# Two fused transformer blocks on one core: work of the first microseconds shared out among three engines, and three waits before matmuls put in another order

## The chip, the cores and the metric

The kernel runs on one NeuronCore of a Trainium2 chip: a matrix engine (TensorE, PE in the profile), a vector engine (VectorE, DVE), an activation engine (ScalarE, ACT), a general one (GpSimd, POOL) and a sync engine (SyncE, SP) which here only issues transfers. Each engine runs its own instructions in program order; what must come after work on another engine waits for a semaphore. The metric is the time of one execution on the device in microseconds (us); the time of a kernel is the median of its runs.

## What is computed

Two blocks follow each other on one sequence of 256 tokens of width 1024. All is fp32. Block 1 is a feed-forward half step, a mixer (attention beside a gated unit) and another feed-forward half step, with a norm ahead of each and one behind the last; block 2 has two layers and carries 256 context tokens beside the 256 latent ones. Cut to what matters here:

```python
def modulate_2(x, gain, shift, scale):
    return rms_norm(x, gain) * (1 + scale) + shift

def swiglu_2(h, w_in, w_out):
    a, b = jnp.split(h @ w_in, 2, axis=-1)
    return (jax.nn.silu(a) * b) @ w_out

def hyena_filter(...):                       # depends on no token, only on the filter's weights
    h = jnp.sin(freq * (emb @ fw1 + fb1))    # three sine layers of 64 x 256
    h = jnp.sin(freq * (h @ fw2 + fb2))
    h = jnp.sin(freq * (h @ fw3 + fb3))
    ...                                      # @ fw4, times a decay window: the taps
mod_l = (silu(c) @ w_mod[i] + b_mod[i])      # 216 chunks of 128 modulation values in all, from 1024 x 128 weights each
x_lat = x_lat + 0.5 * mod_l[:, 2] * swiglu_2(modulate_2(x_lat, ...), ffn_a_in[i], ffn_a_out[i])
x_ctx = x_ctx + 0.5 * mod_c[2] * swiglu_2(modulate_2(x_ctx, ...), ffn_a_in[i], ffn_a_out[i])
return first_block's rmsnorm(h, norm_final)  # its output is the latent x of block 2
```

## The kernel before

**Phases.** The list PHASES gives the order: for block 1 b1_gu1, b1_down1 (feed-forward 1), b1_in, b1_out (mixer), b1_gu2, b1_down2 (feed-forward 2); for block 2 l0_gu1 to l0_down2 (layer 0) and l1_gu1 to l1_down2 (layer 1). A phase streams its weights in blocks (128x2048, or 128x1408 in a down phase). For each block SP loads `raw`, ACT writes the high part `whi` (`hi_static`, `hi_loop`; L614, L619), DVE the rest `wlo` = raw − whi (`lo_static`, `lo_loop`; L1755, L1760), and PE does three matmuls per product (`three`, L1024 to L1026: high×high, high×low, low×high). raw, whi and wlo have two buffers each, so block n+2 can't be converted before PE has left block n. Activations are split the same way: Yh by ACT, Yl by DVE, for hidden ones Hh by ACT and Hl by POOL (L487). PE leaves the results in the banks pg0 and pg1 of its accumulation memory, px0 and px1 hold smaller things.

**A norm** goes through all engines: ACT squares a chunk (SQ), POOL or PE sums them, PE adds over the partitions (`total`, L1091), ACT takes the root (L651), DVE the reciprocal (L1897), PE spreads it over the partitions (`turn_back`, L1109), DVE scales a chunk (TMP, L1918), ACT writes Yh (L658), DVE Yl (L1909), eight chunks in all; PE takes them as they come.

**The start.** SP loads 16 modulation units (128x1024 each, ADA), then the first two raw blocks, in that order. PE multiplies the sine layers (L1195), DVE brings each argument into range (L2016 to L2022), ACT takes the sine (L701). DVE works the units in between (L1768: product with c, which lies in px1, and sum in one instruction): two after each layer, three more, and after the taps the last seven. PE makes the taps (L1201), DVE windows them (HN, L2031) and forms sums and differences (HP, L2034); PE adds up the squares of x for norm b1_0, then multiplies HP with a Fourier matrix (L1210), DVE keeps the result (HF, L2041), and POOL writes it to HBM for later use ("spectrum", L492). Before the first product DVE also makes the two first `wlo`.

**The context tokens' norm and the merge.** Block 1 has only latent tokens; the context ones join at l0_gu1. Their squares and sums are made by POOL after the whole of b1_gu2 (15 operations, L518 to L523, into RS); PE adds them up (`ctx_sums`, L1117) after the fourth of 16 blocks of b1_down2 and spreads the root (`ctx_spread`) after the eighth; the scaling (L1949), Yh (L716) and Yl of context chunk c stand in the block loop of b1_down2 (`ctx_y`, `ctx_hi`) at its steps 6 to 13. `merged_start` opens l0_gu1: PE multiplies block 0 with the context half while block 1's final norm and the first norm of block 2 are still being made (on ACT `merged_norm`: L724, L726, then `second("l0_gu1")`, the high part of block 1), then the second block, then the latent half.

**l1_out** adds up 16 chunks of retention output, OH and OL, in pairs k = 0 to 7. PE takes them for its first two weight blocks in an order written by hand; pair k needs `ret_lo` k+1 (DVE, L2441).

```python
for u in range(2):                                  # L1718
    ...
    for k in range(7):
        if u == 0:
            pe.wait_ge(sem["ret_lo"], k + 1)
        l1_out_block(out_base + u, u, (2 * k, 2 * k + 1))
pe.wait_ge(sem["ret_lo"], 8)
for u in range(2):
    l1_out_block(out_base + u, u, (14, 15))
```

## Time and profile before

| | us |
|---|---|
| median of 3 runs | 2589.26 (2585.46 to 2595.65) |
| the profiled execution, its own time | 2586.83 |
| its span (first to last record) | 2585.1 |
| PE busy in it | 2463.7 |
| DVE, ACT, POOL busy | 1517.6, 881.6, 408.5 |

A row of a timeline gives the start in us, the duration (of all its instructions together, where x2 or more), the engine, the line, the operation with out<-in and their shapes, and in brackets how long the engine had been idle before it and which engine's work released it. PEclk in a window is the share of the full clock (2.4 GHz) at which TensorE ran: 1.00, or 0.50 for 1.2 GHz.

### The profile page before, as it was taken

To read this page: it belongs to the slowest core of one execution; us is meant where nothing else is said; L and a number is where in the kernel's file an instruction comes from. 1 tells how busy PE (TensorE), PEld (TensorE's weight loads), DVE (VectorE), ACT (ScalarE), POOL (GpSimd) and SP (SyncE) were. 2 spreads that over 40 slices of the span, in tenths; PEclk is the share of its full clock that TensorE was granted. 3 is DMA by queue.
4 is the path that set the end of the run, shared out by engine and by line. 5 is a ranking of instruction groups with operands and counts; after the bars stand their busy time and mean duration, and the time that the engine had idled before them with its cause. 6 is when DMAs were issued, how large, how long until landed. Compare 5 with 4: busy or idle time off the path is not lost.

```text
span 2585.1 us, 38719 instructions
## 1 busy us (share of the span) xinstructions
PE 2463.7 (95%) x14366; PEld 2153.8 (83%) x14366; DVE 1517.6 (59%) x2440; ACT 881.6 (34%) x1070; POOL 408.5 (16%) x376
## 2 busy tenths in 40 slices
PE   6998889988999998999999999999999999998999
PEld 4998769988888886877778888878888789998999
DVE  7676557975877766245567776642222265554544
ACT  2443444435322223333232222232222232244443
POOL 0110532131111102432221111011110111001110
PEclk6999888999999999999999999999999999999999
DMA  7778544854555544211135555422222332134454
GB/s 271 266 259 288 206 155 154 270 201 155 184 190 189 186 162 170 74 69 57 47 112 196 191 177 191 165 81 97 97 82 89 114 126 72 66 115 161 163 176 165
DMA packets 79727, 400.08 MB, mean 155 GB/s; under 512 B 8800, under 2 KB 12896, under 8 KB 54432
## 3 DMA queue, kind: packets, MB, share of 16 engines
q1 hardware_dynamic: 77216, 393.39, 43.7%
q0 software_dynamic: 784, 3.15, 0.3%
q10 hardware_dynamic: 1648, 2.47, 0.3%
q8 instruction: 51, 0.84, 0.1%
q14 instruction: 28, 0.23, 0.0%
HBM read 396.88 MB, written 2.10 MB: 154 GB/s over the span
## 4 chain that ended last, share of the span: by engine, by line
PE 82%; DVE 7%; ACT 3%; DMA 3%; issue 2%; POOL 1%; ACTq 0%; SPq 0%; DVEq 0%; POOLq 0%
PE pg L1024 24%; PE pg L1026 23%; PE pg L1025 23%; DMA raw<-w_d 2%; PE pg L1083 2%; PE pg L1085 1%; PE pg L1084 1%; DMA raw<-w_t 1%; PE px L1684 1%; DVE Yl L1909 1%; DVE wlo L1755 1%; ACT whi L614 1%; ACT whi L619 1%; DVE wlo L1760 1%; DVE TMP L1918 1%
## 5 line engine op out<-in xcount | busy, mean ns | idle before, releaser
L1024 PE MATMUL pg<-Yh,whi 128*128 128x256 f32 (+1 forms) x2808 | 955.1, 340 | 38.1 <-DVE Yl L1909 21.3
L1025 PE MATMUL pg<-Yl,whi 128*128 128x256 f32 (+1 forms) x2808 | 944.5, 336 | 0.0
L1026 PE MATMUL pg<-Yh,wlo 128*128 128x256 f32 (+1 forms) x2808 | 943.8, 336 | 0.0
L1760 DVE TENSOR_TENSOR wlo<-raw,whi 128x2048 fp32r<-128x2048 f32 (+1 forms) x202 | 415.5, 2057 | 547.1 <-ACT whi L619 546.1
L1024 PEld LDWEIGHTS pg<-Yh,whi 128*128 128x128 f32 x2808 | 542.6, 193 | 105.0 <-issue 32.1
L1025 PEld LDWEIGHTS pg<-Yl,whi 128*128 128x128 f32 x2808 | 543.2, 193 | 51.5
L1026 PEld LDWEIGHTS pg<-Yh,wlo 128*128 128x128 f32 x2808 | 542.6, 193 | 52.2
L619 ACT ACTIVATE whi<-raw 128x2048 fp32r<-128x2048 f32 (+1 forms) x202 | 348.5, 1725 | 585.5 <-PE pg L1026 554.9
L1024 PE MATMUL pg<-Hh,whi 128*128 128x256 f32 (+1 forms) x1056 | 358.5, 339 | 7.9 <-DVE wlo L1760 4.4
L1025 PE MATMUL pg<-Hl,whi 128*128 128x256 f32 (+1 forms) x1056 | 356.0, 337 | 0.0
L1026 PE MATMUL pg<-Hh,wlo 128*128 128x256 f32 (+1 forms) x1056 | 356.0, 337 | 0.0
L487 POOL TENSOR_TENSOR Hl<-TMP,Hh 128x256 f32 (+1 forms) x132 | 134.6, 1020 | 1007.0 <-ACT Hh L634 1007.0
L1794 DVE CUSTOM_DVE_ANT_0 ada<-ada,px 128x1024 f32<-128x1024 f32 x200 | 243.7, 1219 | 10.3 <-DMA ada<-w_ada 4.9
L1024 PEld LDWEIGHTS pg<-Hh,whi 128*128 128x128 f32 x1056 | 199.7, 189 | 36.1 <-DVE wlo L1760 6.4
L1025 PEld LDWEIGHTS pg<-Hl,whi 128*128 128x128 f32 x1056 | 199.0, 188 | 24.6
L1026 PEld LDWEIGHTS pg<-Hh,wlo 128*128 128x128 f32 x1056 | 199.0, 188 | 24.3
L614 ACT ACTIVATE whi<-raw 128x2048 fp32r<-128x2048 f32 (+1 forms) x66 | 113.4, 1719 | 243.4 <-PE pg L1026 125.7
L1755 DVE TENSOR_TENSOR wlo<-raw,whi 128x2048 fp32r<-128x2048 f32 (+1 forms) x58 | 116.8, 2015 | 125.3 <-ACT whi L614 125.3
L634 ACT ACTIVATE Hh<-TMP 128x256 f32 (+3 forms) x132 | 69.5, 526 | 335.8 <-DVE TMP L1863 335.8
L503 POOL TENSOR_TENSOR wlo<-raw,whi 128x512 fp32r<-128x512 f32 x88 | 111.3, 1296 | 178.7 <-ACT whi L850 117.7
L464 POOL TENSOR_TENSOR TMP<-TMP,SQ 128x512 f32<-128x512 f32 (+1 forms) x56 | 60.6, 1082 | 401.2 <-ACT SQ L683 331.3
L1791 DVE CUSTOM_DVE_ANT_0 RS<-ada,px,small 128x512 f32<-128x512 f32 x144 | 107.7, 748 | 5.1
(316 smaller groups left out, 2366.6 us busy)
## 6 DMA issues: line engine op xcount, KB each, us to landing
raw<-w_t SPq DMA_DIRECT2D x194, 1024.0 KB, 4.9
ada<-w_ada SPq DMA_DIRECT2D x200, 512.0 KB, 3.5
raw<-w_d SPq DMA_DIRECT2D x96, 704.0 KB, 4.0
ADA<-w_ada SPq DMA_DIRECT2D x16, 512.0 KB, 16.8
NB<-na_bias POOLq DMA_DIRECT2D x8, 256.0 KB, 3.0
X<-x_t ACTq DMA_DIRECT2D x1, 1024.0 KB, 23.8
spectrum<-HF POOLq DMA_DIRECT2D x1, 1024.0 KB, 8.8
X<-ctx_t SPq DMA_DIRECT2D x1, 1024.0 KB, 7.2
```

The source lines that it names most:

```text
L487: pool.tensor_tensor(Hl[:, bass.ds(j * 2 + u, 1), 0:tokens], TMP[:, u:u + 1, 0:tokens], Hh[:, bass.ds(j * 2 + u, 1), 0:tokens].bitcast(F32 ...
L503: ins = pool.tensor_tensor(wlo[:, n % 2, part], raw[:, n % 2, part], whi[:, n % 2, part].bitcast(F32), ALU.subtract)
L614: act.activation(whi[:, n % 2, 0:size], raw[:, n % 2, 0:size], ACT.Copy).then_inc(sem["hi_ready"], 1)
L619: act.activation(whi[:, n % 2, 0:size], raw[:, n % 2, 0:size], ACT.Copy).then_inc(sem["hi_ready"], 1)
L634: act.activation(Hh[:, bass.ds(j * 2 + u, 1), 0:tokens], TMP[:, u:u + 1, 0:tokens], ACT.Copy)\
L1024: pe.matmul(out, w_hi, y_hi, start=first, stop=False)
L1025: pe.matmul(out, w_hi, y_lo, start=False, stop=False)
L1026: return pe.matmul(out, w_lo, y_hi, start=False, stop=last)
L1755: dve.tensor_tensor(wlo[:, n % 2, 0:size], raw[:, n % 2, 0:size], whi[:, n % 2, 0:size].bitcast(F32), ALU.subtract)\
L1760: dve.tensor_tensor(wlo[:, n % 2, 0:size], raw[:, n % 2, 0:size], whi[:, n % 2, 0:size].bitcast(F32), ALU.subtract)\
L1791: summed(dve.tensor_tensor_reduce(RS[:, :], ada[:, n % 2, 512:1024], px[1][:, 1, :], 1.0, part, ALU.mult, ALU.add, total[:, 0:1]), 2)
L1794: summed(dve.tensor_tensor_reduce(w, w, px[2 - streams][:, :, :], 1.0, 0.0, ALU.mult, ALU.add, total[:, streams - 1:streams]), 1 if stream ...
```

## The change

It has four parts.

**A, the start.** ACT copies the spread c from px1 into memory (CS). POOL multiplies units 1, 3, 5, 7, 9, 11 and 13 with CS (L533 of after), and ACT adds each up (`unit_sum`, an activation with an accumulated sum, and a 128x1 one for the bias): three of them between the sines, four behind the root of norm b1_0, around the two first high parts. DVE keeps nine units. HP moves from DVE to POOL. The products with the Fourier matrix leave the start. The `wlo` of block 1 moves behind the eight Yl of norm b1_0. A semaphore now tells of two units' loads instead of one, and raw block 0 is loaded before unit 13.

**B, norm b1_1** (behind b1_down1). PE does the Fourier products here, 16 of 128x256 in four groups: two ahead of the totals, one ahead of `turn_back`, one behind it. ACT keeps the groups (`keep_spectrum`, 128x2x256 each): two ahead of the root, two behind the eight Yh. POOL issues the write to HBM, now of 1024 rows of 1 KB, behind its part of the high and low split of b1_in's second block.

**C, context and merge.** The 15 POOL operations move into b1_gu2's hidden loop, one behind each of the steps 4 to 18, with their sums in TMP instead of RS. `ctx_sums` comes after the second block of b1_down2, `ctx_spread` after the fourth; root and reciprocal at step 2; scaling at steps 4 to 11, Yh at 5 to 12, Yl at 6 to 13, so that a chunk's three operations no longer stand in one step. In `merged_start` the totals come first, and the spread before the second half of the context product; ACT does `second("l0_gu1")` ahead of the two roots; at the last step of b1_down2 DVE adds to X before it makes the `wlo` of l0_gu1's block 0.

**D, l1_out.** Block 0 takes pairs 0 to 5, block 1 pairs 0 to 2, block 0 pairs 6 and 7, block 1 pairs 3 to 7.

The diff, cut to its core:

```diff
+POOL_UNITS = (1, 3, 5, 7, 9, 11, 13)
+DVE_UNITS = (0, 2, 4, 6, 8, 10, 12, 14, 15)
...
+                if n == 13:
+                    sp.dma_start(raw[:, 0, :], w_t[0, :, :]).then_inc(sem["raw0_in"], 16)
+                sp.dma_start(first_unit(n), w_ada[n, :, :]).then_inc(sem[f"ada_first{n // 2}"], 16)
...
+                        if m >= 4 and m < 19:
+                            ctx_squares(m - 4)
...
+            for k, n in enumerate(POOL_UNITS):
+                pool.wait_ge(sem[f"ada_first{n // 2}"], 32)
+                pool.tensor_tensor(first_unit(n), first_unit(n), CS[:, :], ALU.mult).then_inc(sem["pool_unit"], 1)
...
+                if name == "b1_0":
+                    unit_sum(3)
+                    unit_sum(4)
+                    hi_static(0, BLK)
+                    unit_sum(5)
+                    unit_sum(6)
+                    hi_static(1, BLK)
...
+            def unit_sum(k):
+                n, total = POOL_UNITS[k], small[:, 40 + k:41 + k]
+                act.wait_ge(sem["pool_unit"], k + 1)
+                act.activation(first_unit(n), first_unit(n), ACT.Copy, accum_out=total).then_inc(sem["unit_sum"], 1)
+                act.wait_ge(sem["unit_sum"], k + 1)
+                act.activation(MOD[:, n, 0:1], total, ACT.Identity, bias=...)
...
                     if name == "b1_down2":
-                        four(0)
+                        four(0, (0,))
                         ctx_sums()
-                        four(1)
+                        four(0, (1,))
                         ctx_spread()
...
-                first_units(2 * layer, 2 * layer + 1)
-            first_units(6, 7, 8)
+                first_units(2 * layer)
+            first_units(6, 8)
...
+            dve.wait_ge(sem["unit_done"], len(POOL_UNITS))
```

ACT at the start of the program, before (FS is a sine, SQ the squares of x, whi the two first high parts):

```order
L701 ACTIVATE FS<-FA 64x256 x3
L644 ACTIVATE SQ<-X 128x256 x8
L614 ACTIVATE whi<-raw 128x2048 x2
L648 ACT_TABLE_LOAD
L651 ACTIVATE small<-px,small 128x2
L658 ACTIVATE Yh<-TMP,MOD 128x256 x8
```

The same engine and place after, from behind the third sine's unit (ADA_80 and ADA_81 are unit buffers):

```order
L678 ACTIVATE SQ<-X 128x256 x8
L680 ACT_TABLE_LOAD
L686 ACTIVATE small<-px,small 128x2
L751 ACTIVATE ADA_80,small<-ADA_80 128x1024
L753 ACTIVATE MOD<-small,V 128x1
L751 ACTIVATE ADA_80,small<-ADA_80 128x1024
L753 ACTIVATE MOD<-small,V 128x1
L648 ACTIVATE whi<-raw 128x2048
L751 ACTIVATE ADA_81,small<-ADA_81 128x1024
```

The root (L651, now L686) has moved ahead of the high parts, and four unit sums stand around these.

ACT where block 1 meets block 2, before (L724 and L726 are the two roots, the second L614 is block 1 of l0_gu1):

```order
L614 ACTIVATE whi<-raw 128x2048
L672 ACT_TABLE_LOAD
L683 ACTIVATE SQ<-X 128x256
L685 ACTIVATE SQ<-X,V 128x256
L724 ACTIVATE small<-pg,small 128x2
L726 ACTIVATE small<-small 128x2
L614 ACTIVATE whi<-raw 128x2048
```

After:

```order
L648 ACTIVATE whi<-raw 128x2048
L717 ACT_TABLE_LOAD
L728 ACTIVATE SQ<-X 128x256
L730 ACTIVATE SQ<-X,V 128x256
L648 ACTIVATE whi<-raw 128x2048
L791 ACTIVATE small<-pg,small 128x2
L793 ACTIVATE small<-small 128x2
```

The high part of block 1 (L614, now L648) stands ahead of the roots now.

POOL after its hidden loop of b1_gu2, before (RS takes the context's squares and sums):

```order
L518 TENSOR_TENSOR RS<-X 128x256
L521 TENSOR_TENSOR RS<-X 128x256
L523 TENSOR_TENSOR RS<-RS 128x256
```

After, within the hidden loop (Hl is the low part of a hidden chunk, TMP takes squares and sums):

```order
L501 TENSOR_TENSOR Hl<-TMP,Hh 128x256
L520 TENSOR_TENSOR TMP<-X 128x256
L501 TENSOR_TENSOR Hl<-TMP,Hh 128x256
L524 TENSOR_TENSOR TMP<-X 128x256
L501 TENSOR_TENSOR Hl<-TMP,Hh 128x256
L526 TENSOR_TENSOR TMP<-TMP 128x256
```

One context operation stands behind each hidden chunk instead of all behind the last.

## Rows read from the trace of the kernel before

**Rows 1.** Timeline of PE at the start: taps, sums of squares, first product.

```profile
23.64 7.19 PE L1201 MATMUL pg<-FW,FS 64*128 64x512 f32 x8 [4.42 <-ACT FS L701]
30.77 6.99 PE L1091 MATMUL px<-ones,SQ 128*128 128x1 f32 x32
55.48 0.55 PE L1024 MATMUL pg<-Yh,whi 128*128 128x256 f32 x1 [1.73 <-DVE Yl L1909]
```

**Rows 2.** Timelines of DVE and ACT at the start: unit, third argument, low parts; block 0 done.

```profile
13.39 1.21 DVE L1768 CUSTOM_DVE_ANT_0 ADA<-ADA,px 128x1024 f32<-128x1024 f32 x1
...
22.86 0.28 DVE L2022 TENSOR_SCALAR FA<-FA 64x256 f32<-64x256 f32 x1
...
45.46 4.48 DVE L1755 TENSOR_TENSOR wlo<-raw,whi 128x2048 fp32r<-128x2048 f32 x2
...
63.24 1.91 ACT L619 ACTIVATE whi<-raw 128x2048 fp32r<-128x2048 f32 x1 [0.98 <-PE pg L1026]
```

**Rows 3.** The units' loads (tile ADA, issues from 2.2 to 9.9 us).

```profile
DMA to landing us min/median/max: 7.4/15.7/20.8
```

**Rows 4.** Timelines of POOL and DVE where both read memory at once, and alone.

```profile
560.44 1.88 POOL L521 TENSOR_TENSOR RS<-X 128x256 f32<-128x256 f32 x1
...
563.24 0.62 POOL L521 TENSOR_TENSOR RS<-X 128x256 f32<-128x256 f32 x1
```

**Rows 5.** DVE at the same time, and two operations of 128x128 beside POOL and alone.

```profile
560.22 1.63 DVE L1760 TENSOR_TENSOR wlo<-raw,whi 128x1408 fp32r<-128x1408 f32 x1 [1.74 <-ACT whi L619]
...
337.19 2.23 DVE L2085 TENSOR_SCALAR P<-P,small 128x128 f32<-128x128 f32 x2
...
344.49 0.55 DVE L2085 TENSOR_SCALAR P<-P,small 128x128 f32<-128x128 f32 x2
```

**Rows 6.** Groups by form on POOL: busy us, mean ns of one.

```profile
L487 POOL TENSOR_TENSOR Hl<-TMP,Hh 128x512 f32 x66 | 85.6, 1297 | 657.4 <-ACT Hh L634 657.4
L487 POOL TENSOR_TENSOR Hl<-TMP,Hh 128x256 f32 x66 | 49.0, 743 | 349.5 <-ACT Hh L634 349.5
```

**Rows 7.** Timelines of PE and ACT at norm b1_1; issue of the spectrum's write.

```profile
258.20 1.02 PE L1091 MATMUL pg<-ones,SQ 128*128 128x1 f32 x4 [4.65 <-ACT SQ L683]
...
270.10 1.28 ACT L795 ACT_TABLE_LOAD   x1
271.77 1.91 ACT L753 ACTIVATE whi<-raw 128x2048 fp32r<-128x2048 f32 x1 [0.39 <-PE pg L1026]
...
L492 POOL DMA_DIRECT2D spectrum<-HF x1: 733/733/733, 52.5 to 52.5; - x1
```

**Rows 8.** Timeline of PE at ctx_sums.

```profile
576.06 1.01 PE L1117 MATMUL pg<-ones,RS 128*128 128x1 f32 x4 [6.33 <-POOL RS L523]
```

**Rows 9.** Windows: us, then PE, PEld, DVE, ACT, POOL busy (x), PEclk, DMA share, GB/s.

```profile
436.00:536.00 100.00, 100.00 (x835) 100.00 (x835) 94.45 (x158) 44.69 (x52) 12.84 (x18) 1.00 0.81 273
...
578.00:580.00 2.00, 2.00 (x11) 2.00 (x11) 0.00 (x0) 0.00 (x0) 1.25 (x1) 0.50 0.00 0
...
600.00:620.00 20.00, 18.99 (x158) 18.41 (x156) 11.68 (x15) 11.66 (x16) 3.89 (x3) 1.00 0.50 179
646.00:648.00 2.00, 2.00 (x12) 2.00 (x11) 1.78 (x5) 1.21 (x3) 0.00 (x0) 0.50 0.00 0
```

**Rows 10.** Timelines of PE, ACT and POOL at the merge.

```profile
630.52 0.36 PE L1024 MATMUL pg<-Yh,whi 128*128 128x256 f32 x1 [1.99 <-issue]
...
643.77 0.58 PE L1024 MATMUL pg<-Yh,whi 128*128 128x256 f32 x1 [4.59 <-POOL wlo L477]
...
636.43 1.90 ACT L614 ACTIVATE whi<-raw 128x2048 fp32r<-128x2048 f32 x1
...
638.41 5.31 POOL L477 TENSOR_TENSOR wlo<-raw,whi 128x512 fp32r<-128x512 f32 x4 [11.54 <-ACT whi L614]
```

**Rows 11.** Timelines of PE and ACT at l1_out's first blocks.

```profile
2349.09 0.38 PE L1024 MATMUL pg<-OH,whi 128*128 128x256 f32 x1 [4.12 <-DVE X L1876]
...
2344.33 1.91 ACT L619 ACTIVATE whi<-raw 128x2048 fp32r<-128x2048 f32 x1 [6.44 <-PE pg L1026]
```

More of the change, by code:

```diff
@@ L660, in norm @@
                     ins.then_inc(sem["y_hi"], 1)
+                if name == "b1_1":
+                    keep_spectrum(2)
+                    keep_spectrum(3)
             def squares(name):
@@ L722, in merged_norm @@
                 r, base, _ = NORMS["final"]
+                second("l0_gu1")
                 act.wait_ge(sem["square_used"], base + 8 + CREDIT)
@@ L726, in merged_norm @@
                 act.activation(small[:, 18:20], small[:, 22:24], ACT.Sqrt, bias=small[:, 0:1], scale=1.0 / D).then_inc(sem["rms_ready"], 1)
-                second("l0_gu1")
                 for c in range(8):
@@ L1043, in product, with four @@
                     h_before = KF * [f.replace("gu", "down") for f in FFNS].index(name) + CREDIT
-                    def four(j):
-                        for v in range(2):
+                    def four(j, pairs=(0, 1)):
+                        for v in pairs:
                             pe.wait_ge(sem[evac], j * 2 + (ebase + v - 2 + 1))
@@ L1158, in merged_start @@
                 m.then_inc(sem["rms_spread"], 2)
+                for kt in range(8):
+                    part(0, 1, kt, ctx)
                 pe.wait_ge(sem["lo_ready"], n + CREDIT + 2)
@@ L1835, in body @@
                             units(name, j * per, u)
-                        if last:
+                        if last and name == "b1_down2" and u >= per - 2:
+                            evac(j, u)
+                            if u == per - 1:
+                                lo_static(BASE["l0_gu1"], BLK)
+                        elif last:
                             n = base + u + 2 + per * j
```

211 lines of the change are left out of this document (124 added, 87 removed).

## The prediction

> **What bounds the kernel now.** The page's first part puts PE at 95% of the span (2463.7 of 2585.1); DVE, ACT and POOL have room on average. So an edit pays only where PE waits, or where it runs at half its clock behind a wait. I read the timelines of PE for its idle time in brackets, then the timeline of the engine named there. The change touches six such places: the start, where the first product begins at 55.48 [rows 1]; norm b1_1, 4.65 us idle [rows 7]; `ctx_sums`, 6.33 [rows 8]; the second half of b1_down2, where PE is busy 18.99 of 20 us at the full clock [rows 9]; the merge, 1.99 and 4.59 [rows 10]; and l1_out, 4.12 [rows 11]. In b1_gu2 PE is busy 100 of 100 us [rows 9]: there the change can only cost.
>
> **Part A, the start.** Before, the third sine argument ends at 23.1 (22.86 + 0.28 [rows 2]), the taps run from 23.64 for 7.19 us, the norm's sums then for 6.99 [rows 1]. Of the two units between sine layers each takes 1.21, and 1.38 with its two small operations, until the next begins at 14.77 [rows 2]. Behind the sums come what is left of the units, the two `wlo` (4.48 from 45.46 [rows 2]), HF and the first scaling. Block 0's product follows the eight Yl chunks and is done at about 63.1, where ACT takes up the next high part [rows 2].
>
> If nothing gets in the way: one unit less in each of two gaps brings the argument to 20.3, the taps' end to 28.7 (X lands about then) and the sums' end to 35.8; the root is at 36.2. ACT then has four unit sums and two high parts. A high part is 1.91 [rows 2]; for a unit sum I take 1.45: half a high part and half a microsecond for the bias operation and the waits. The loads land in the order of issue, the twelfth 20.8 after it [rows 3], so the last pairs and raw 0 by 34 to 38, in time; with four times 1.45 and twice 1.91 behind the root the second high part ends at 46.0, Yh begins, and the first product starts at 47.1, block 1's `wlo` ends at 55.6: **−7.5** against 63.1.
>
> But POOL now multiplies seven units beside the sine chain. Its product has two operands in memory and 1024 elements per partition. By [rows 6] 256 elements cost 0.743 and 512 cost 1.297, so 0.554 per 256 more: 2.4 for 1024 (I take 2.35; ends 2.2 and 2.6). And the timelines show what it does to a neighbour [rows 4, 5]: the POOL product of 560.44 takes 1.88 instead of 0.62, ending only after the DVE `wlo` of 560.22, which has two operands in memory, and DVE's two operations of 128x128 take 2.23 beside POOL and 0.55 alone. One of the two waits for the whole of the other. The range reduction is such work: five of its seven operations per layer read and write memory alone. The units DVE keeps are not (their second operand is in px1). The Trainium skill says the same (SBUF — State Buffer, "SBUF: two separate sides"): the port pair shared by VectorE and GpSimd is an exclusive lock held for a whole instruction, taken by VectorE's two-port modes and by its operations with two memory operands. By that rule, which speaks against this change, the sum below for A is right; if it didn't hold, −7.5 would be.
>
> POOL gets its units at 9.7, 15.4, 19.3, 22.5, 25.9 and 29.2, each just as a sine layer is at work. I follow the chain: such a product delays the layer it meets by 2.3, 1.2, 2.35, 0.3, 2.35 and 2.35, together 10.8, since a longer chain meets more of them. The third argument ends at 31.8 (21.0 + 10.8), the taps at 39.5, the sums at 46.5; ACT's queue behind the root then sets the first product at 57.5 and `wlo` of block 1 ends at 66.0: **+2.9** against 63.1. Ends: −2.3 with 2.2 per product and luck in the meetings, +4.7 with 2.6.
>
> **Part B, norm b1_1.** The first two Fourier groups take 1.73 each at the full clock and fall into PE's 4.65 of idle before 258.20 [rows 7], hidden; `keep_spectrum` 0 and 1 before the root (0.6 each) lie under them in part; if that cover is gone they cost 1.2. Groups 2 and 3 run while PE waits for the root and the first Yl, at best free. The two kept behind the Yh push ACT's table load and the next high part (271.77, which waited 0.39 for PE [rows 7]) by about 1.2 − 0.4, and the first products at half clock may end a little sooner for PE having been busy. I take **+1.0**, ends 0 and +4. POOL's issue of a write of 1024 rows has no equal here: that of 128 rows takes 0.73 [rows 7], so between 0.73 and eight times that, 5.9. Behind it on POOL stands the low part of b1_in's third block, 2 to 3 us off: hence up to +4. SP, whose mix loads now wait for the fourth group, gets them out some 10 us before they are used.
>
> **Part C.** *Sums.* `ctx_sums` no longer waits for 15 POOL operations that began only at 559.7 and collided with the `wlo` [rows 4, 5]: 6.33 idle goes [rows 8]. Behind it PE ran until about 582 at half clock (0.50 at 578 to 580 [rows 9]), 11 matmuls where 20 would fit; over those 5 us almost half was lost, 2.4. What comes late next: root (with a table load of 1.28 [rows 7]), reciprocal and spread must fit into the two blocks before `ctx_spread`'s place, each of 33 matmuls at 0.12 (835 in 100 us [rows 9]), 3.9 us; with a high part of 1.4 ahead of them they take some 3.3. **−8.7**, ends −7.5 and −9. *Pace.* From 600 to 620 PE lacks 1.01 of 20 [rows 9]; over the steps 6 to 13, with the three operations of a chunk no longer chained in one step, I put a pair of blocks at 7.8 instead of 8.5, three and a half times: **−2.4**, ends −0.5 and −2.8. *Merge.* `second` ahead of the roots starts the high part at about 631 instead of 636.43, and POOL's low part (5.31, four operations) comes before PE needs it: of 4.59 none remains [rows 10]. The 1.99 before 630.52 falls to about 1.1, by the add to X before the `wlo` and by the totals first. The latent part ran at 0.50 (646 to 648 [rows 9]) from 643.8 to 649.8 behind that wait, 2.5 of it lost. 4.6 + 0.9 + 2.5: **−8.0**, ends −5 (the next wait is the Yl of the latent half, near) and −8.5. *In b1_gu2.* Fifteen POOL operations of 0.7 stand behind the hidden ones. POOL has 12.84 busy of 100 [rows 9]; they fall beside the unit sums, whose operand is in px1, and end about 1 us before the next `wlo`. Cost **0**; DVE is busy 94.45 of 100, so a miss is felt (rival 3).
>
> **Part D, l1_out.** Both first blocks end together, so the next high part begins only at 2344.33, its low part and the X add follow, and PE, 4.12 idle, goes on at 2349.09 [rows 11]. In the new order 24 matmuls of block 1 (its pairs 3 to 6) no longer stand ahead of block 0's end, 2.9 at 0.12 each [rows 9], and the wait for pair 6's OL is spent on block 1's first pairs: together about 4.1. So block 0 is done at 2340.1, its successor's high part is there at 2342.1, the low part at 2344.4, the X add just before 2344.95, where PE goes on: 4.1 sooner. Of the some 3 us at half clock that follow the wait before (11 matmuls in 2 us instead of 20 [rows 9]), 1.4 goes if the shorter wait of 1.9 that is left doesn't bring them back. **−5.5**, ends −4 and −6.
>
> **Sum.** +2.9 + 1.0 − 8.7 − 2.4 − 8.0 − 5.5 = −20.7. The profiled execution took 2586.83, so 2566.1; the median of the runs lies 2.43 above it: **2568.5**.
>
> **Rivals.** *1, no blocking at the start.* POOL and DVE pass each other there: A is −7.5 and the sum −31.1, **2558**. For it: the small sine operations have 64 partitions and are short; against it, [rows 4, 5]. *2, POOL's product is slowed, not only queued.* The product of 560.44 took three times its time alone [rows 4]. If that holds of each of the seven, 2.35 × 3 = 7.1, the chain waits for POOL and ACT's sums for the last product. Following the chain with 5 us per product gives +24.6, with 6 +33.6, so at 7.1 +43.5; the rest stays −23.6: **2609**, slower. It decides from 4.9 us per product on. Against it: both rows of that kind fit simple waiting. *3, collisions in b1_gu2.* With the phase of POOL's operations 1 us later, each of 15 holds up a `wlo` by up to 0.74, and DVE has no slack: +11, **2579.5**, no change that can be told. *4, gains come back as other waits* (PE loses to raw loads or to DVE what A, C and D save), the sum halved: about **2579** too.
>
> **Chances.** Forecast 0.63, rival 1 0.18, rival 2 0.05, rivals 3 and 4 0.07 each. The range takes in rival 1 and rivals 3 and 4, with their bounds: the ends of the terms give −28.6 to −8.3 for the forecast, 2560.6 to 2580.9; rival 1 reaches 2555. So 2554 to 2581. About 0.5%, 13 us, is what a measurement of this kernel can tell from no change. Faster by more (under 2576.3): forecast, rival 1 and a little of rivals 3 and 4, 0.84. Within: 0.11. Slower by more: 0.05.
>
> **What would show it.** A: FA operations of DVE at 1 to 2.5 us beside POOL's products, and the first product near 57.5; at 47 rival 1 is right, beyond 75 rival 2. B: block 0 of b1_in ending within 1 us of its old distance from the totals. C: idle before `ctx_sums` under 0.5 and PEclk 1.00 behind it; no idle before block 1 of l0_gu1. b1_gu2 still 100 of 100. D: no wait for the X add behind the second block. The prediction is wrong if the first product comes far from 57.5, if C's waits turn up elsewhere in b1_down2, or if b1_gu2 shows gaps.

## The result

The changed kernel takes 2574.22 us (median of 6 runs, 2571.64 to 2580.97) where the kernel before takes 2589.54 (6 runs): ratio 0.9943, 95% interval 0.9921 to 0.9964. Run again in another series it gave 0.9958 (0.9943 to 0.9972). It is some 11 to 15 us faster; 20.7 were forecast, with a range that holds the measured time. The direction was right, the size was not, and the terms erred both ways.

The page of the changed kernel, first the engines' busy time, then the share of each engine in the chain that ended last:

```profile
PE 2459.0 (96%) x14382; PEld 2151.6 (84%) x14382; DVE 1507.4 (59%) x2415; ACT 893.7 (35%) x1097; POOL 423.3 (16%) x385
...
PE 85%; DVE 6%; DMA 3%; ACT 3%; issue 2%; SPq 0%; POOL 0%; ACTq 0%; DVEq 0%; POOLq 0%
```

PE is busy 4.7 us less than before although it has 16 more records. The span is 14.0 us shorter, so the other 9.3 us are waits of PE that are gone. Where the time went can be read with one trick: take the same ACT instruction in both traces (a high part, a sine, a root) and subtract its two start times. Where this difference steps, time was won or lost. Beside it stand the forecast's terms. The first column is the time in the trace before, the next three are the difference to it at that place, all in us. The third of them is the kernel before itself in a second trace (run e9_before): it shows how far two traces of one kernel lie apart.

```
place in the trace before             changed   same, 2nd trace   before, 2nd trace   forecast for the step
  69   second block of b1_gu1            -1.7         -1.9               +1.0          A      +2.9
 252   end of b1_down1                   -1.5         -1.0               +1.4
 282   b1_in, block 3                    +4.8         +6.2               +1.4          B      +1.0
 541   end of b1_gu2                     +4.5         +7.6               +4.4          (b1_gu2: 0)
 583   b1_down2, behind ctx_sums         -4.9         -1.2               +4.3          C sums -8.7
 626   end of b1_down2                   -7.8         -4.7               +4.3          C pace -2.4
 696   l0_gu1                           -12.9        -11.2               +3.0          C merge -8.0
1015   norm ahead of l0_in              -13.0        -11.1               +4.4
1335   l0_gu2                            -7.8         -5.8               +8.5          (nothing)
2308   end of l1_in                      -7.1         -5.1               +8.4
2357   l1_out                           -12.4        -10.6               +8.3          D      -5.5
2563   last down phase                  -13.7        -12.7               +6.1
```

A and B are far off, with opposite signs; C's sums, its pace and D are right within 0.7 us in the first trace and 1.1 in the second; the merge is 1.5 to 2.9 short; and 5.2 and 5.4 us are lost between 1015 and 1335, where the change touches no line.

Against the last column much of this last loss goes away. The kernel before, unchanged, loses 4.1 us over the same stretch in its second trace, and run e11_merge_alone, which has only a small part of the change, loses 4.1 too. So the first trace of the kernel before is a quick one there, and the changed kernel loses only 1.1 to 1.3 us against the other two. The same holds at the start: e9_before stands at +1.0 and e11_merge_alone at +1.4, so against them part A gives −2.7 to −3.2 instead of −1.7 and −1.9. Between 282 and 541 the two lose 3.0 us each. At the steps of B, of the sums, of the pace and of l1_out they agree with the first trace within 0.2 us (0.6 at the sums in e11_merge_alone), so these terms can be read from one trace.

**The start (A).** Timelines of POOL and DVE, where they meet in the second sine layer, and the first product on PE, all of the changed kernel:

```profile
14.55 2.35 POOL L533 TENSOR_TENSOR ADA<-ADA,CS 128x1024 f32<-128x1024 f32 x1 [2.35 <-DMA ADA<-w_ada]
17.96 2.51 POOL L533 TENSOR_TENSOR ADA<-ADA,CS 128x1024 f32<-128x1024 f32 x1 [1.06 <-DMA ADA<-w_ada]
```

```profile
14.26 1.21 DVE L1847 CUSTOM_DVE_ANT_0 ADA<-ADA,px 128x1024 f32<-128x1024 f32 x1
...
17.40 3.35 DVE L2098 SCALAR_TENSOR_TENSOR FA<-FK,FA 64x256 f32<-64x256 f32 x3
```

```profile
28.34 7.19 PE L1271 MATMUL pg<-FW,FS 64*128 64x512 f32 x8 [5.65 <-ACT FS L758]
35.46 6.99 PE L1157 MATMUL px<-ones,SQ 128*128 128x1 f32 x32
43.09 1.22 PE L1179 MATMUL px<-ident,small 128*128 128x128 f32 x4 [0.64 <-DVE small L2114]
53.02 0.55 PE L1090 MATMUL pg<-Yh,whi 128*128 128x256 f32 x1 [8.71 <-DVE Yl L1986]
```

The three range-reduction steps take 3.35 instead of 1.32, because POOL's product of 17.96 stands in their way. A step that reads only one operand in memory can be held too (this one takes 0.28 elsewhere; POOL's product beside it runs from 9.86 to 12.20):

```profile
10.46 1.88 DVE L2095 TENSOR_SCALAR FK<-FA 64x256 f32<-64x256 f32 x1
```

DVE's unit at 14.26, whose second operand is in px1, takes its usual 1.21 although POOL works beside it. The first product starts at 53.02. Before it was 55.48 [rows 1], and 57.5 was forecast.

**Norm b1_1 (B).** Timelines of SP, ACT and PE:

```profile
264.65 0.44 SPq L369 DMA_DIRECT2D SBI<-sgu_b  x1
265.14 0.91 SPq L349 DMA_DIRECT2D ada<-w_ada  x2
266.08 0.69 SPq L365 DMA_DIRECT2D raw<-w_t  x1
```

```profile
269.36 1.28 ACT L861 ACT_TABLE_LOAD   x1
276.11 1.91 ACT L819 ACTIVATE whi<-raw 128x2048 fp32r<-128x2048 f32 x1 [5.47 <-DMA raw<-w_t]
```

```profile
278.35 0.58 PE L1090 MATMUL pg<-Yh,whi 128*128 128x256 f32 x1 [8.38 <-ACT GU L831]
```

Before, ACT took this high part at 271.77 and waited 0.39 for PE [rows 7]. Now ACT is ready at 270.6 and waits 5.47 for the raw block itself. SP issued its load at 266.08, behind the six loads for the mixer, which wait for the fourth Fourier group. Before the change it was issued at 257.70.

**`ctx_sums` and the pace (C).** Timeline of PE, and windows with the columns of [rows 9]:

```profile
565.28 0.50 PE L1188 MATMUL pg<-ones,TMP 128*128 128x1 f32 x4
573.70 0.71 PE L1195 MATMUL pg<-ident,small 128*128 128x128 f32 x4
```

```profile
569.00:571.00 2.00, 2.00 (x19) 2.00 (x18) 0.21 (x1) 1.58 (x3) 0.74 (x2) 1.00 0.54 124
...
440.00:540.00 100.00, 100.00 (x835) 100.00 (x835) 94.46 (x156) 44.57 (x52) 20.79 (x30) 1.00 0.82 272
590.00:610.00 20.00, 19.92 (x169) 19.75 (x170) 14.18 (x20) 13.08 (x17) 2.60 (x2) 1.00 0.55 181
```

Neither row has an idle time in brackets: the 6.33 of [rows 8] are gone, the clock behind them is full, and the pace is 19.92 busy of 20 instead of 18.99. In b1_gu2 POOL is busy 20.79 us of 100 instead of 12.84 and PE still 100 of 100.

**The merge and l1_out.** Timeline of PE:

```profile
622.38 1.02 PE L1210 MATMUL pg<-ones,TMP 128*128 128x1 f32 x8 [0.67 <-DVE X L1952]
...
624.58 0.55 PE L1090 MATMUL pg<-Yh,whi 128*128 128x256 f32 x1 [0.17 <-DVE wlo L1833]
...
650.45 0.49 PE L1090 MATMUL pg<-Yh,whi 128*128 128x512 f32 x1 [0.73 <-DVE TMP L1939]
```

```profile
2338.24 0.38 PE L1090 MATMUL pg<-OH,whi 128*128 128x256 f32 x1 [1.27 <-DVE X L1952]
```

The wait of 1.99 [rows 10] has become 0.67 ahead of the totals and 0.17 ahead of the context product. The 4.59 ahead of block 1 is gone: no row of PE between 624.58 and 650.45 has an idle time in brackets. The 4.12 of l1_out [rows 11] has become 1.27.

### The profile page after: what moved, and what is told of

It is laid out like the page before. It is cut to its first block, busy times and chain, and to the rows that moved or that the text cites. A ratio compares the mean times of both kernels' runs of the same rounds, so it can differ in the third digit from the quotient of the medians.

```text
span 2571.1 us, 38673 instructions
## 1 busy us (share of the span) xinstructions
PE 2459.0 (96%) x14382; PEld 2151.6 (84%) x14382; DVE 1507.4 (59%) x2415; ACT 893.7 (35%) x1097; POOL 423.3 (16%) x385
## 4 chain that ended last, share of the span: by engine, by line
PE 85%; DVE 6%; DMA 3%; ACT 3%; issue 2%; SPq 0%; POOL 0%; ACTq 0%; DVEq 0%; POOLq 0%
PE pg L1090 24%; PE pg L1092 24%; PE pg L1091 24%; DMA raw<-w_t 2%; PE pg L1149 2%; PE pg L1151 1%; PE pg L1150 1%; DMA raw<-w_d 1%; PE px L1764 1%; DVE Yl L1986 1%; DVE wlo L1833 1%; ACT whi L648 1%; DVE TMP L1995 1%; DVE ada L1873 1%; PE px L1527 1%
## 5 line engine op out<-in xcount | busy, mean ns | idle before, releaser
L509 POOL TENSOR_TENSOR Hl<-TMP,Hh 128x512 f32 (+1 forms) x110 | 117.9, 1072 | 901.7 <-ACT Hh L668 901.7
L648 ACT ACTIVATE whi<-raw 128x2048 fp32r<-128x2048 f32 (+1 forms) x66 | 113.4, 1718 | 242.6 <-PE pg L1092 126.4
## 6 DMA issues: line engine op xcount, KB each, us to landing
ADA<-w_ada SPq DMA_DIRECT2D x16, 512.0 KB, 15.4
X<-x_t ACTq DMA_DIRECT2D x1, 1024.0 KB, 28.2
```

The costliest lines, as they stand in the source:

```text
L509: pool.tensor_tensor(Hl[:, bass.ds(j * 2 + u, 1), 0:tokens], TMP[:, u:u + 1, 0:tokens], Hh[:, bass.ds(j * 2 + u, 1), 0:tokens].bitcast(F32 ...
L648: act.activation(whi[:, n % 2, 0:size], raw[:, n % 2, 0:size], ACT.Copy).then_inc(sem["hi_ready"], 1)
```

## The experiments

Most are the changed kernel with one edit; e8_best and e10_late_sharing have several, e9_before is the kernel before as it is, and e11_merge_alone is the kernel before with one part of the change. All medians and ratios are against runs of the kernel before on the same chip; differences of a few us between two kernels are read from the traces, stage by stage, as above.

### The changed kernel once more

> The changed kernel again, beside the others on the same chip. Theory (the losses seen in its first trace are made by the order of its instructions): the same waits return, the first product at 53.0 us, the first product of b1_in's second half at 278.4 behind 8.4 us idle, ratio to the kernel before 0.994. The one loss that I hold for chance is the half clock of PE at l0_in from 1017 to 1024 (8.45 us for a block that took 5.77 before, behind the same wait of 3.03): it may be there or not.

2578.42 us (median of 10 runs), ratio 0.9958 (0.9943 to 0.9972). The waits came back: the first product at 52.84, PE's wait in b1_in 7.22 (8.38 in the first trace), the mixer's block at +6.2, `ctx_sums` without a wait, the stretch behind 1015 losing 5.4. It is the second column of the table. So the loss at l0_in, which I had held for chance, is there again.

### B: where the 8.4 us come from

```diff
-                    if b == 1:
+                    if b == 2:
                         sp.wait_ge(sem["taps_spectrum"], 4)
```

> The changed kernel with one edit on SP: the six loads for the mixer, which wait for the fourth group of Fourier products, are issued behind the load of raw block 2 of b1_in instead of ahead of it. Theory 1 (that raw load, issued at 266.1 instead of 257.7 behind them and 10.0 us on its way, makes the 8.38 us wait of PE): the raw load is issued at about 257, ACT takes the high part at about 271 right behind its table load, PE waits 2 to 3 us, the block starts at 272 to 273.5 instead of 278.35: 5 to 6 us less in all, about 2568.5. Theory 2 (the wait comes from ACT's queue, where two copies of the spectrum now stand ahead of the table load): the wait falls by less than 1 us. Theory 3 (the loads are bound by bandwidth, 99% from 262 to 275): the raw block comes earlier, but the units' or the next blocks' loads later, and half of the gain is lost by 290.

2571.68 us, ratio 0.9940 (0.9922 to 0.9958). The raw load is issued at 257.36 and the high part starts right behind the table load (ACT, then PE):

```profile
270.50 1.28 ACT L861 ACT_TABLE_LOAD   x1
271.79 1.91 ACT L819 ACTIVATE whi<-raw 128x2048 fp32r<-128x2048 f32 x1
...
274.03 0.58 PE L1090 MATMUL pg<-Yh,whi 128*128 128x256 f32 x1 [2.92 <-ACT GU L831]
```

At block 3 of b1_in the kernel stands at +0.5 against the trace before, instead of +4.8 and +6.2: 4.3 and 5.7 us less, about what theory 1 expected (5 to 6); the median came out at 2571.68, not at 2568.5. Theory 2 falls: with the two copies of the spectrum still in ACT's queue, the wait is 2.92 (2.33 before the change). By the end of the mixer the kernel had lost 2.6 us again, which looked like theory 3; but the unedited kernel lost 2.0 there in its second trace and won 0.7 in its first, and the kernel before lost 3.8 in its second. So this stretch, whose raw blocks wait behind units' loads in SP's queue, scatters by some 4 us by itself, and theory 3 can be neither seen nor excluded.

Without that order on SP the norm thus costs 0.8 us (from −0.3 ahead of it to +0.5), near the term's 1.0; and POOL's issue of 1024 rows took 1.05, near the lower of the two bounds (0.73 and 5.9):

```profile
269.65 1.05 POOL L543 DMA_DIRECT2D spectrum<-HF  x1 [4.45 <-ACT HF L765]
```

### A: does DVE wait for a whole POOL instruction?

```diff
-                pool.tensor_tensor(first_unit(n), first_unit(n), CS[:, :], ALU.mult).then_inc(sem["pool_unit"], 1)
+                for q in range(4):
+                    part = slice(256 * q, 256 * q + 256)
+                    ins = pool.tensor_tensor(first_unit(n)[:, part], first_unit(n)[:, part], CS[:, part], ALU.mult)
+                ins.then_inc(sem["pool_unit"], 1)
```

> The changed kernel with each POOL product of 128x1024 made in four pieces of 128x256. Theory (DVE's sine work waits for a whole POOL instruction): no sine operation waits more than some 0.7 us at a time; each argument loses about 1 instead of 2 us, the third ends at 25 to 26 instead of 27.8; X lands at 33.0, so of the 2 to 3 us at most 2.4 reach the first product (50.6 to 52), total -1.5 to -2.4. Rival (DVE and POOL share the memory by turns, so the pieces don't matter): the same 1.6, 2.2 and 2.2 us lost, nothing gained.

2572.69 us, ratio 0.9935 (0.9918 to 0.9951). The three steps beside POOL take 2.14 instead of 3.35 (1.32 alone), POOL's product 3.05 instead of 2.51:

```profile
16.90 2.14 DVE L2101 SCALAR_TENSOR_TENSOR FA<-FK,FA 64x256 f32<-64x256 f32 x3
...
17.99 3.05 POOL L535 TENSOR_TENSOR ADA<-ADA,CS 128x256 f32<-128x256 f32 x4 [0.55 <-DMA ADA<-w_ada]
```

The size of POOL's instruction sets the size of each wait, so DVE does wait for the whole of one. In sum it brings little. The taps start at 27.03 instead of 28.34, and the first product at 51.71 instead of 53.02, but the first sine layer had also begun 0.8 sooner (9.08 instead of 9.89), so about 0.5 of the 1.3 is the splitting's. More small waits take the place of few long ones: in the second layer the steps ahead of the three and behind them now take 0.70 each where they take 0.28 alone.

### A: the same start without the sharing

```diff
-POOL_UNITS = (1, 3, 5, 7, 9, 11, 13)
-DVE_UNITS = (0, 2, 4, 6, 8, 10, 12, 14, 15)
+POOL_UNITS = ()
+DVE_UNITS = tuple(range(16))
...
-                first_units(2 * layer)
-            first_units(6, 8)
+                first_units(2 * layer, 2 * layer + 1)
+            first_units(6, 7, 8)
...
-            first_units(10, 12)
+            first_units(9, 10, 11, 12, 13)
```

(ACT's copy of c and its unit sums go too.)

> The changed kernel without the sharing out: DVE makes all 16 units, as before the change, ACT and POOL none; the Fourier products stay behind the first down phase, HP stays on POOL. Theory (the sharing costs more than it brings, the gain of the start is that the Fourier products and HF have left it): the third argument ends at 23.1 again, the taps at 31, X lands at about 33, the sums end at 40, DVE is done with the units at 43 to 43.5 and with the first low part at 45.7; the first product starts at 47 to 48 instead of 53.0, block 1's low part ends at 55.5 to 56.5 instead of 61.2: -5, about 2569. Rival (the forecast's own picture: without POOL and ACT the units hold DVE back beyond 50): first product at 53 or later, no gain.

2568.73 us, ratio 0.9922 (0.9906 to 0.9939). Timeline of PE:

```profile
23.97 7.19 PE L1264 MATMUL pg<-FW,FS 64*128 64x512 f32 x8 [4.42 <-ACT FS L752]
33.48 6.99 PE L1150 MATMUL px<-ones,SQ 128*128 128x1 f32 x32 [2.32 <-ACT SQ L678]
...
48.36 0.55 PE L1083 MATMUL pg<-Yh,whi 128*128 128x256 f32 x1 [6.04 <-DVE Yl L1979]
```

The first product starts at 48.36 (expected 47 to 48), and the kernel stands at −6.3 behind the start against −1.7: the sharing costs 4.7 us, counted at the first product.

These 4.7 have two parts, read from the two traces (no run takes away one of them alone). The spread of the root (`px<-ident,small`) starts at 43.09 in the changed kernel and at 41.11 here: 2.0 come through the sine chain, whose other delay is covered by the wait for x. The other 2.7 arise behind the root, and there they come from ACT's unit sums. In the changed kernel two of these, 1.37 each, stand ahead of each high part, and Yh begins the moment the second high part is done; here both high parts are done at 44.4 and ACT waits 2.81 for DVE. ACT in the changed kernel, then here:

```profile
49.94 1.90 ACT L648 ACTIVATE whi<-raw 128x2048 fp32r<-128x2048 f32 x1
51.85 0.91 ACT L700 ACTIVATE Yh<-TMP,MOD 128x256 fp32r<-128x256 f32 x2
```

```profile
40.69 3.70 ACT L648 ACTIVATE whi<-raw 128x2048 fp32r<-128x2048 f32 x2
47.19 0.91 ACT L696 ACTIVATE Yh<-TMP,MOD 128x256 fp32r<-128x256 f32 x2 [2.81 <-DVE TMP L1988]
```

What won at the start is work that left DVE ahead of the first product. In the kernel before, DVE was busy up to 52.2, with these two and the second `wlo` (2.24, half of the 4.48 of [rows 2]) among it:

```profile
33.49 2.36 DVE L2034 TENSOR_TENSOR HP<-HN 128x1024 f32<-128x1024 f32 x2
...
49.86 2.35 DVE L2041 TENSOR_SCALAR HF<-pg 128x1024 f32<-128x1024 f32 x2
```

The three add up to 7.0, and the first product comes 7.1 sooner. No run takes one of them alone.

The 2.32 in the second row of PE is the wait for x, which lands at 33.0 where it landed at 28.6 before the change. The Fourier matrix, loaded ahead of x on ACT's queue, now comes in 512 pieces of 1 KB; in the changed kernel it lands at 19.8 instead of 16.4. That the pieces make the delay is likely, but no run changes them alone. In the changed kernel the later taps cover it.

### Three edits together, and sharing at another time

> Three edits together: all 16 units on DVE (as in e4_dve_units), the mixer's loads behind raw block 2 of b1_in (as in e1_mix_loads), and x loaded ahead of the Fourier matrix on ACT's queue. Theory: the edits are at different places and add up. In e4 x landed at 33.0 and the taps were done at 31, so with x at 27 to 29 the sums start 1 to 2 us sooner, but DVE's 16 units end at 43 whatever x does: the first product stays at 47 or comes half a us earlier. e4 gave -6.5 at the end of b1_in against the changed kernel, e1 -1.4 to -2.9: together -8 to -9, 2565 to 2567, ratio 0.990 to 0.991. Rival (both live off the same slack of the loads in b1_in, which are held back there by units not yet reduced): no better than e4, ratio 0.992.

```diff
-            act.dma_start(DF0, dft[:, 0:2].rearrange("p a b n -> p (a b) n")).then_inc(sem["dft_in"], 16)
             act.dma_start(X[:, :, 0:256], x_t).then_inc(sem["x_in"], 16)
+            act.dma_start(DF0, dft[:, 0:2].rearrange("p a b n -> p (a b) n")).then_inc(sem["dft_in"], 16)
```

2564.30 us, ratio 0.9900 (0.9883 to 0.9916). x lands at 25.4, the first product starts at 47.25, block 3 of b1_in stands at −5.9 and l0_gu1 at −25.4. The gains add up and the rival falls: at block 3 of b1_in e4_dve_units stands at −2.2 and e1_mix_loads at +0.5.

> As e8_best, but three units (7, 9, 11) go to POOL after the third sine argument, when DVE does nothing that reads two operands in memory, and ACT adds them up between the second and the third square, while PE is at the taps. Theory (sharing as such pays; what costs in the changed kernel is POOL beside the sine chain, and ACT's sums between the root and the high parts): the third argument ends at 23.1 as in e8, POOL's products at 2.35 each are done at 30.5, DVE has four units behind the taps instead of seven and is done at 39, the first low part at 42, the first scaling at 42.4 instead of 45.56, the first product at 44.1 instead of 47.25: -3, total 2561, ratio 0.989. Rival (the start is bound by x, the root or the loads by then): the first product at 46 to 47, nothing gained.

```diff
+POOL_UNITS = (7, 9, 11)
...
             pool.wait_ge(sem["c_kept"], 1)
+            pool.wait_ge(sem["sine_arg"], 3)
...
                     for c in range(k):
+                        if name == "b1_0" and c == 2:
+                            for s in range(3):
+                                unit_sum(s)
```

2561.96 us, ratio 0.9884 (0.9863 to 0.9904): the best median of all, 12 to 16 us below the changed kernel's and 28 below that of before. Its interval overlaps that of e8_best, so the gain against e8_best is read from the start in the traces. POOL, then PE:

```profile
23.94 6.99 POOL L534 TENSOR_TENSOR ADA<-ADA,CS 128x1024 f32<-128x1024 f32 x3 [22.92 <-DVE FA L2098]
```

```profile
31.42 6.98 PE L1156 MATMUL px<-ones,SQ 128*128 128x1 f32 x32
39.65 1.22 PE L1178 MATMUL px<-ident,small 128*128 128x128 f32 x4 [1.24 <-DVE small L2113]
44.65 0.55 PE L1089 MATMUL pg<-Yh,whi 128*128 128x256 f32 x1 [3.78 <-DVE Yl L1985]
```

Three products of 2.33 each, none slowed, and the first product at 44.65 (expected 44.1), with its first sine 0.7 later than in the kernel with three edits. Behind the start it stands at −9.9 against −7.4. Sharing pays where POOL doesn't meet DVE's sine work and ACT's sums don't stand between the root and the high parts. This run changes both at once (and shares three units, not seven), so it doesn't tell which of the two saved how much.

### D: l1_out

```diff
-            for u, pairs in ((0, range(0, 6)), (1, range(0, 3)), (0, range(6, 8)), (1, range(3, 8))):
+            for u, pairs in ((0, range(0, 7)), (1, range(0, 7)), (0, range(7, 8)), (1, range(7, 8))):
```

> The changed kernel with the old order of pairs in l1_out (part D undone). Theory (the 5.3 us between 2300 and 2356 come from this order alone): PE waits 1.5 and 4.1 again and the tail comes 5.3 us later against the rest of the program. Rival (they come from the clock, which was at half behind the wait): under 2.

One run, 2584.75 us. Timeline of PE:

```profile
2336.78 0.38 PE L1090 MATMUL pg<-OH,whi 128*128 128x256 f32 x1 [1.50 <-DVE OL L2519]
2347.98 0.57 PE L1090 MATMUL pg<-OH,whi 128*128 128x256 f32 x1 [4.12 <-DVE X L1952]
```

Both waits are back to the hundredth, and from 2308 to 2357 the kernel loses 1.0 us against the trace before where the changed one wins 5.3 to 5.5: the order is worth 5.3 to 5.5 counted against the trace before and 6.3 to 6.5 against this one, and the rival (only clock) falls.

### C: the parts of it

ACT's high part behind the roots again:

```diff
-                second("l0_gu1")
                 act.wait_ge(sem["square_used"], base + 8 + CREDIT)
...
+                second("l0_gu1")
                 for c in range(8):
```

> The changed kernel with ACT's high part of l0_gu1's block 1 behind the two roots, as before the change. Theory (of part C's merge, this order is most of the gain): POOL's low part starts at about 629.5 instead of 625.0 and ends at 634.5; PE, which reaches it after three context products at about 633, waits 1 to 3 us with the clock full or half behind it: 1 to 4 us later in all. Rival (the gain comes from the totals and the spread going first, and POOL's low part is in time either way): no wait, same time within 0.5.

One run, 2578.94 us. POOL's low part starts at 634.70 and PE waits 1.39 at 640.13, at full clock. From 626 to 696 this kernel wins 6.0 against the trace before, the changed one 5.1 and, in its second trace, 6.5: the wait that the theory expected (1 to 3 us) is there, but the order on ACT is worth no more than two traces of one kernel differ, near the rival. The other moves of the merge (totals, spread, the add to X) carry the gain; no run parts these three. The start of this run shows something else:

```profile
13.85 2.38 POOL L533 TENSOR_TENSOR ADA<-ADA,CS 128x1024 f32<-128x1024 f32 x1 [1.64 <-DMA ADA<-w_ada]
...
14.06 2.32 DVE L2099 TENSOR_SCALAR FA<-FA 64x256 f32<-64x256 f32 x1
```

The code is that of the changed kernel there, but the unit landed 0.7 us sooner, and POOL began 0.2 before the last step of the first sine layer instead of 0.3 after the next unit had begun. The first product came at 55.71, not 53.02. So the sharing makes the start depend on when a load lands, by 2.7 us here. Seven traces have the seven products of POOL at the start. In the five others without an edit there the first product lies between 52.79 and 53.61.

The context's operations behind the hidden loop again:

```diff
-                        if m >= 4 and m < 19:
-                            ctx_squares(m - 4)
+                    for m in range(15):
+                        ctx_squares(m)
```

> The changed kernel with the context's 15 POOL operations behind b1_gu2's hidden loop again, everything else as changed. Theory (ctx_sums' wait was made by these operations): they run from about 562 to 574, ctx_sums, which now comes after two blocks instead of four, waits 8 to 10 us, the clock falls behind it; 9 to 13 us later in all. If instead b1_gu2 is faster without them (a hidden cost of their place in it), blocks there take less than 5.7 us each; I expect no difference there (under 0.3 us over the phase).

One run, 2586.96 us. PE and a window of b1_gu2:

```profile
578.58 1.01 PE L1188 MATMUL pg<-ones,TMP 128*128 128x1 f32 x4 [11.50 <-POOL TMP L526]
```

```profile
440.00:540.00 100.00, 100.00 (x836) 100.00 (x835) 94.47 (x155) 44.22 (x51) 12.62 (x17) 1.00 0.83 270
```

The wait is 11.50 (expected 8 to 10), and the loss from 541 to 583 is 14.6 us against the changed kernel (+5.2 where that has −9.3), above my 9 to 13. b1_gu2 is equally fast with the 15 operations and without: their place costs nothing, as the forecast had it.

### The merge alone, and the clock at l0_in

One loss was held by no term: behind the second block of l0_in PE waits 3.03 us in every trace. In the trace before the clock stays up, in the changed kernel it falls behind the wait. First two windows of the kernel before, then two of the changed one, the wait and what follows it:

```profile
1028.00:1030.00 2.00, 0.00 (x0) 0.00 (x0) 0.00 (x0) 2.00 (x3) 0.73 (x1) 1.00 0.00 0
1030.00:1032.00 2.00, 1.79 (x8) 1.49 (x9) 0.00 (x0) 1.14 (x3) 2.00 (x3) 1.00 0.00 0
```

```profile
1015.00:1017.00 2.00, 0.00 (x0) 0.00 (x0) 0.00 (x0) 2.00 (x3) 0.34 (x1) 0.89 0.00 0
1017.00:1019.00 2.00, 1.40 (x3) 1.16 (x4) 0.00 (x0) 1.52 (x4) 2.00 (x2) 0.50 0.00 0
```

> The kernel before, once more, for a second trace. In all nine traces of kernels with the change PE takes about 2.7 us longer over the first blocks of l0_in than in the one trace of before, though the code there is the same, and 1.7 longer in the two stages up to l0_out. Theory (the clock's steps there fall by chance, and the first trace of before was lucky): the second trace shows the half clock behind the 3.03 us wait and the 2.7 us too. Rival (the change makes them, by what it moved in time): the second trace is as the first, within 0.3 us, at both places.

One run, 2593.01 us. At l0_in it is as the first trace of before (0.2 us off, no half clock), which speaks for the rival there. But between 1082 and 1270 it loses 3.2 against the first trace, and so does e11_merge_alone, while the changed kernel loses 1.7 there. The cause shows in the clock: the profile shows PE busy all the time in both traces, at the full clock in the first (upper row), at half of it for some 6 of 8 us in the second (lower row; an estimate from its 0.62).

```profile
1084.00:1092.00 8.00, 8.00 (x46) 5.85 (x45) 3.30 (x7) 5.26 (x9) 0.60 (x1) 1.00 0.22 83
```

```profile
1089.00:1097.00 8.00, 8.00 (x22) 5.23 (x21) 3.30 (x7) 3.62 (x6) 0.60 (x1) 0.62 0.20 67
```

So the first trace of before was a lucky one in this stretch, as the theory had it; at l0_in it was not.

> The kernel before with the merge's new order alone: ACT's high part of l0_gu1's block 1 ahead of the two roots, PE's totals ahead of the context product and the spread ahead of its second half, DVE's add to X ahead of the first low part. Two questions. The size of this term: the changed kernel gave 5.2 to 6.6 us there where 8.0 was forecast; I expect 5 to 6.5 between the entry to the last down block and l0_gu1's second pair of blocks, total 0.9975. And the clock at l0_in: theory (its step falls behind the 3.03 us wait depending on where the earlier steps were, and a shift in the merge is enough to move it): this kernel shows the half clock there and loses 2.7 us back, like the ten with the whole change. Rival (it hangs on something else in the change, or on chance): full clock there, as in both traces of before.

The edit moves `second("l0_gu1")`, the totals, the spread and the add to X as in the change, nothing else. 2586.01 us (10 runs), ratio 0.9982 (0.9970 to 0.9993). The merge alone wins 7.0 us from 626 to 696 (and 8.0 up to 658) against the first trace of before, more than the 5 to 6.5 expected and near the forecast's 8.0. The second trace of before, though, wins 1.3 over the same stretch with no change at all: against it the merge alone is worth 5.7 and the changed kernel's merge 3.9 and 5.3. At l0_in the clock stays up: the theory that a shift in the merge moves the step falls.

In all ten traces of the changed kernel and its variants, from 25 us early to 1 us late at that place, the first blocks of l0_in lose 3.0 to 3.4 us; in the three others nothing or 0.2. It isn't the chip, since e9_before and e10_late_sharing ran on the same one. Nor is one of these parts needed for it: the seven shared units (e4_dve_units, e8_best lack them), the order in l1_out (e5_l1_order), that on ACT in the merge (e6_second_late), the place of the context's operations (e7_ctx_late). What the ten have in common are the Fourier products in norm b1_1, the new steps of b1_down2, the other moves of the merge and the layout in memory. Which of these does it, or whether it is chance after all, stays open.

## Why the forecast was right in direction and off in size

**A, forecast +2.9, measured −1.7 and −1.9** (−2.7 to −3.2 against the other two traces without part A). The mechanism was right: the sine work waits for POOL's products, whole instructions, at the 2.35 us each that the row of [rows 6] gave. The term that was mis-sized is the count. The forecast let six products meet the chain, two of them in part, together 10.8 us. In the trace the chain loses 1.60 in the first layer, 2.24 in the second and 2.21 in the third, 6.1 in all. POOL began its products at 9.86, 14.55, 17.96, 21.32, 24.73 and 28.14, about 1 us sooner than the forecast had followed them (9.7, 15.4, 19.3, 22.5, 25.9, 29.2). They come 3.4 us apart and a layer with its unit takes 6.1 to 6.8, so about every second product falls beside DVE's unit, which it doesn't disturb. The third argument so ends at 27.8 instead of 31.8, which is 4.0 of the 4.5 us by which the first product came sooner than forecast (53.0, not 57.5).

The Trainium skill (SBUF — State Buffer, "SBUF: two separate sides") says both: that the loser waits for the whole instruction, and that VectorE's work with at most one operand in memory is left alone, except in its two-port modes, which a `tensor_scalar` can enter. The trace agrees, with 1.21 for the unit beside POOL, 1.32 grown to 3.35 for the three steps with two operands, and 0.28 grown to 1.88 for the `tensor_scalar` of 10.46. Following the count was the weak step, not the rule.

Smaller slips of the forecast lie in the same part. It lets the chain without meetings end at 20.3 for its −7.5 and at 21.0 for its +2.9; in the trace this is 21.7 (27.8 − 6.1), since the first layer began 0.65 later than before. Six of the seven operations of a layer read and write memory alone, not five. x was to land at about 28.7 and landed at 33.0, which the taps covered.

**B, forecast +1.0, measured +6.2 and +7.2.** The step that failed is the sentence on SP: "gets them out some 10 us before they are used" looked at the six loads that were moved and not at the one queued behind them. The raw load of the next block stood there and went out 8.4 us later, and ACT had to wait 5.47 for it. e1_mix_loads shows it by taking that alone away: the step falls to 0.8, near the term's 1.0. The forecast's other worry, POOL's issue, cost 1.05.

**C and D.** The sums came to −9.3 and −8.8 (forecast −8.7), the pace to −2.9 and −3.5 (−2.4), l1_out to −5.3 and −5.5 (−5.5). The merge came to −5.1 and −6.5 in the changed kernel and to −7.0 alone (−8.0). The changed kernel's first trace has PE at half clock from 624 to about 627.5, its second has not: that fits the difference of 1.4 between the two. A further loss is DVE's, which in l0_gu1 makes its units before the next low part and is late by 0.73 now that PE comes sooner; this wait stands in the first trace alone.

**The rivals.** Number 1 (no blocking) and 2 (slowed products) are both out: products take 2.35 to 2.51, waits are one instruction long. Number 3 is out: 100 of 100 in b1_gu2. Number 4 came true in part: gains came back as another wait (B, 5.2 beyond its term) and as half clock at l0_in (3.0 to 3.4).

The terms A to D sum up to −18.1 in the first trace and −19.0 in the second, where −20.7 were forecast. That they come so near is in part luck: A was 4.6 to 4.8 better than its term, B and the merge together 7.7 to 8.1 worse, and the one makes up for more than half of the other. What no step held are the 5.2 to 5.4 lost between 1015 and 1335, of which two traces without the change lose 4.1 as well, so that about 1 us is left for the change. It is the difference of two things: 3.0 to 3.4 that only kernels with the change lose at l0_in, and some 1.5 less than the other two that they lose between 1082 and 1270. The 1.3 to 2.1 won in the last phases, without a line changed there, are no gain of the change either: the second trace of the kernel before wins 2.1 there. One trace of before was too few to set terms of 1 us against.

## What to carry to other kernels

When an instruction with a wait is put into a queue, look at what stands behind it there, not at whether it is itself in time. Work given to GpSimd beside VectorE costs VectorE nothing only while that does the right kind of work: here the unit, with one operand outside the memory that both share, kept its 1.21 us, while steps with two operands there, and a `tensor_scalar` with one, waited. Then ask also what the third engine must do with the result: of the 4.7 us that sharing seven units cost, 2.0 came through the sine chain and 2.7 from ACT's sums ahead of its high parts. Three units, shared after the sine chain and summed before the root, gave 2.5. A term that is a count of meetings between two engines should be given as a range of counts, since the landing of one load decided 2.7 us here. And before a difference of a few us between two traces is explained, take a second trace of the kernel before: here the two differ by up to 8.5 us, most of it in three stretches.

## What the runs showed of the hardware that I had not expected

- The same wait of 3.03 us before the same code is followed by full clock in three traces and by half clock in ten. Such steps also come with PE busy without a break: from 1089 to 1097 the second trace of the kernel before has a PEclk of 0.62 where the first has 1.00, and from 1082 to 1270 the two differ by 3.2.
- POOL's issue of a write of 1024 rows of 1 KB took 1.05 us, where one of 128 rows took 0.73 [rows 7].
- The same 512 KB in 512 pieces instead of 128 landed 3.4 us later (15.7 us from issue instead of 12.3), and the load behind it on the same queue 4.4 us later (28.2 instead of 23.8), although its own issue took as long (0.75 and 0.74). No run changes the pieces alone.
